# RWKV chunk inverse: four levels on the 32x32 diagonal squares, the last level as two products of the cross block

## What is computed

```python
def step(S, inp):
    r_t, w_t, k_t, v_t, kk_t, b_t = inp
    sa = jnp.einsum('bhij,bhj->bhi', S, -kk_t)
    S = (S * w_t[:, :, None, :] + sa[..., None] * b_t[:, :, None, :]
         + v_t[..., None] * k_t[:, :, None, :])
    return S, jnp.einsum('bhij,bhj->bhi', S, r_t)
...
y = (rwkv7_scan(r_h, heads(decay[:, :, 0]), k_h, v_h, kk, b_h, False)
     + rwkv7_scan(r_h, heads(decay[:, :, 1]), k_h, v_h, kk, b_h, True))
```

## Time and profile before

| | us |
|---|---|
| Median of 3 runs | 3145.51 (3141.09 to 3147.05) |
| The profiled execution | 3141.4 |
| Its span, from the first to the last instruction | 3139.6 |
| Stage `rwkv_mix` in it | about 568 to 987 |
| One turn of the stage in it | 23.4 and more |

### The profile page before, as it was taken

The page is one execution under the profiler, slowest core; times in us unless marked ns, Lnnn a source line. Parts: engine busy times, 40 slices in busy tenths (PEclk is TensorE's granted clock), DMA queues, the critical chain, the costliest instruction groups (busy, mean ns, idle before and its releaser), DMA issues.

```text
span 3139.6 us, 56591 instructions
## 1 busy us (share of the span) xinstructions
PE 2915.1 (93%) x25024; PEld 2375.0 (76%) x25024; DVE 1467.5 (47%) x2046; ACT 1153.1 (37%) x1897; POOL 280.8 (9%) x318
## 2 busy tenths in 40 slices
PE   6986899688888799999999999999999999999997
PEld 5765666578785478888888887787887888888886
DVE  3668676245444454433343325666436533234323
ACT  5665665222223243322332225533234333243222
POOL 1000123444441100000000000000000000000000
PEclk8987899799998799999999999999999999999998
DMA  4320244311100222223222222222322223223222
GB/s 141 123 68 3 90 143 141 84 34 34 34 4 30 92 89 89 93 94 99 96 89 95 99 94 97 85 94 87 101 94 88 94 94 101 94 94 121 100 94 81
DMA packets 99541, 273.07 MB, mean 87 GB/s; under 512 B 8224, under 2 KB 35488, under 8 KB 99296
## 3 DMA queue, kind: packets, MB, share of 16 engines
q1 hardware_dynamic: 90512, 236.93, 22.9%
q0 software_dynamic: 8784, 32.51, 3.1%
HBM read 256.69 MB, written 12.58 MB: 86 GB/s over the span
## 4 chain that ended last, share of the span: by engine, by line
PE 62%; DVE 2%; ACT 1%; DMA 1%; issue 0%; DVEq 0%; ACTq 0%
PE be_ps L2921 45%; PE be_ps L2942 15%; DVE be_ring L2711 1%; PE be_ps L2955 1%; PE be_ps L2663 0%; PE be_ps L2657 0%; ACT be_whi L2988 0%; DMA be_raw<-in_w_out 0%; DVE be_raw_r L3094 0%; DMA be_raw<-in_ple_gate 0%; DVE be_total L2676 0%; DVE ext_r L2721 0%; ACT big L2994 0%; DVE big L2684 0%; DVE big L2693 0%
## 5 line engine op out<-in xcount | busy, mean ns | idle before, releaser
L3094 DVE TENSOR_TENSOR be_raw_r<-be_raw,be_whi 128x1024 fp32r<-128x1024 f32 x361 | 442.4, 1225 | 1002.9 <-ACT be_whi L2988 1002.6
L2921 PE MATMUL be_ps<-ext_r,be_whi 128*128 128x512 f32 x2304 | 714.1, 391 | 15.8 <-PEq L2331 8.6
L2988 ACT CAST be_whi<-be_raw 128x1024 fp32r<-128x1024 f32 x361 | 378.6, 1049 | 895.9 <-DMA be_raw<-in_ffn_down 317.1
L2921 PE MATMUL be_ps<-big_r,be_whi 128*128 128x512 f32 x2048 | 642.2, 394 | 2.4 <-DVE big_r L2719 2.4
L2921 PEld LDWEIGHTS be_ps<-ext_r,be_whi 128*128 128x128 f32 x2304 | 432.5, 188 | 109.0 <-issue 10.2
L2921 PEld LDWEIGHTS be_ps<-big_r,be_whi 128*128 128x128 f32 x2048 | 383.1, 188 | 96.7 <-DVE big_r L2719 3.1
L2921 PE MATMUL be_ps<-ext_r,be_raw_r 128*128 128x512 f32 x1152 | 449.3, 390 | 0.0
L2921 PE MATMUL be_ps<-big_r,be_raw_r 128*128 128x512 f32 x1024 | 407.5, 398 | 0.0
L2942 PE MATMUL be_ps<-ext_r,be_whi 128*128 128x512 f32 x1152 | 354.6, 389 | 0.0
L2921 PEld LDWEIGHTS be_ps<-ext_r,be_raw_r 128*128 128x128 f32 x1152 | 217.0, 188 | 45.3
L2942 PEld LDWEIGHTS be_ps<-ext_r,be_whi 128*128 128x128 f32 x1152 | 216.3, 188 | 45.0
(11 more groups left out here) (328 smaller groups left out, 3886.8 us busy)
## 6 DMA issues: line engine op xcount, KB each, us to landing
be_raw<-in_ffn_gate SPq DMA_DIRECT2D x88, 512.0 KB, 3.5
be_raw<-in_ffn_up SPq DMA_DIRECT2D x88, 512.0 KB, 3.5
be_raw<-in_ffn_down SPq DMA_DIRECT2D x88, 512.0 KB, 3.5
be_raw<-in_conv_in SPq DMA_DIRECT2D x48, 512.0 KB, 3.5
gp_ada<-in_ada POOLq DMA_DIRECT2D x24, 512.0 KB, 3.8
rp_ada<-in_ada POOLq DMA_DIRECT2D x24, 512.0 KB, 3.8
rwkv_prepared<-big SPq DMA_DIRECT2D x16, 512.0 KB, 3.1
be_raw<-in_w_out SPq DMA_DIRECT2D x16, 512.0 KB, 3.6
```

What stands on the lines that cost most here:

```text
L2921: mm = pe.matmul(ps[:, bank], part[:, k * P:(k + 1) * P], xs(k), start=(k == 0 and i == 0), stop=(k == KD - 1 and i == 2))
L2988: act.copy(w.hi[:, n % 3], w.raw[:, n % 3]).then_inc(w.hi_ready, 1)
L3094: dve.tensor_tensor(w.lo(n), w.raw[:, n % 3], w.hi[:, n % 3].bitcast(F32), ALU.subtract).then_inc(w.lo_ready, 1)
```

## The change

Levels 1 to 4 work within the 32x32 squares on the diagonal alone, since all blocks up to 32 rows lie there. `x`, `xt0`, `mx` and the new `xt_sq` hold only these squares (32 columns for each tile in place of 64). Each product of these levels becomes 8 tiles x 4 squares = 32 matmuls, with a stationary operand of 32x32 and 16 moving columns. The fifth level becomes two products of the cross block: the first square's `x` against 32 rows and all 64 columns of `mp` (`cross`), a DVE copy, then the result against the second square's `xt_sq` (`crossed`), and a DVE copy into `xt`. One more DVE operation (`own`) puts the diagonal squares into `xt`. Both products have 16 matmuls, with a stationary operand of 32x64 and 32 moving columns. On POOL `xt0` is made of two halves and their sum. The masks of the levels are half as wide, and only one tile (`cross`, before five of `mx`) is filled with the unit matrix at the stage's start.

```diff
@@ masks @@
-        for n, s in enumerate(LEVELS[1:6]):
-            col = np.arange(CH).reshape(CH // (2 * s), 2, s)[:, d].reshape(1, -1)
-            off = (row // (2 * s) == col // (2 * s)) & (row // s != col // s)
-            out[:, CONST["level_m"] + 2 * n + d] = np.tile(off | (row == col), 4)
+        out[:, CONST["first_rows"], d:d + 1] = p // SQ % 2 == d
+        for n, s in enumerate(LEVELS[1:5]):
+            col = np.arange(SQ).reshape(SQ // (2 * s), 2, s)[:, d].reshape(1, -1)
+            off = (p % SQ // (2 * s) == col // (2 * s)) & (p % SQ // s != col // s)
+            out[:, CONST["level_m"] + n, d * CH:(d + 1) * CH] = np.tile(off | (p % SQ == col), 4)
@@ rwkv_mix, helpers @@
-    levels = range(1, 6)
+    levels = range(1, 5)
+        def cross_one(c, first, d, h, q):
+            at = first + (h * 2 + q) * SQ
+            return ps[chunks[c], LX + d, at:at + SQ]
+        def crosses(first):
+            return ps[:, LX:LX + 2, first:first + 4 * SQ].rearrange("p d (k s) -> p d k s", s=SQ)
+        def square(e):
+            return slice(SQ * e, SQ * e + SQ), slice(SQ * (e % 2), SQ * (e % 2) + SQ)
@@ POOL, first_inverse @@
-                pool.tensor_tensor(xt0[:, :].rearrange("p d h q t -> p d (h q) t"),
-                                   mp[:, par].rearrange("p d h q t -> p d (h q) t"),
-                                   pairs_t.rearrange("p d (a t) -> p d a t", a=1).to_broadcast([P, 2, 4, CH]), ALU.mult
-                                   ).then_inc(*pool_front("xt0"))
+                for name, dst, cols in (("xt0_first", xt0, slice(0, SQ)), ("xt0_more", xt0_more, slice(SQ, CH))):
+                    pool.tensor_tensor(dst[:, :].rearrange("p d h q t -> p d (h q) t"),
+                                       mp[:, par, :, :, :, cols].rearrange("p d h q t -> p d (h q) t"),
+                                       pairs_t[:, :, cols].rearrange("p d (a t) -> p d a t", a=1).to_broadcast([P, 2, 4, SQ]),
+                                       ALU.mult).then_inc(*pool_front(name))
+                pool.wait_ge(*pool_front.by("xt0_more", t))
+                pool.tensor_tensor(flat(xt0), flat(xt0), flat(xt0_more), ALU.add).then_inc(*pool_front("xt0"))
@@ PE, turn @@
-                    for d in two:
-                        for h in heads:
-                            for q in two:
-                                for c, at in enumerate(chunks):
-                                    ins = mm(compact_one(LX, at, 0, n, d, h, q), mp[at, par, d, h, q],
-                                             joined_one(x[at, d, h, q], n, d))
+                    for d, h, q in tiles:
+                        for e in range(4):
+                            rows, cols = square(e)
+                            ins = mm(compact_one(rows, 0, n, d, h, q), mp[rows, par, d, h, q, cols],
+                                     joined_one(x[rows, d, h, q], n, d))
                     ins.then_inc(*pe_made(f"mx{n}"))
...
+                pe.wait_ge(*act_made.by("x4", t))
+                for d, h, q in tiles:
+                    for c in two:
+                        first, _ = square(2 * c + d)
+                        ins = mm(cross_one(c, 0, d, h, q), mp[first, par, d, h, q], x[first, d, h, q])
+                ins.then_inc(*pe_made("cross"))
+                if ahead:
+                    front_v(*divmod(t + 1, n_turns), t + 1)
+                pe.wait_ge(*dve_made.by("cross", t))
+                for d, h, q in tiles:
+                    for c in two:
+                        second, _ = square(2 * c + 1 - d)
+                        ins = mm(cross_one(c, 4 * SQ, d, h, q), cross[second, d, h, q], xt_sq[second, d, h, q])
+                ins.then_inc(*pe_made("crossed"))
+                pe.wait_ge(*pe_made.by("ya0", t))
+                to_output(par, 0, qk)
@@ DVE, turn, behind level 4 @@
+                dve.wait_ge(*pe_made.by("cross", t))
+                dve.tensor_copy(joined(cross[:], 5), crosses(0)).then_inc(*dve_made("cross"))
+                dve.wait_ge(*dve_made.by("xt4", t))
+                dve.tensor_tensor(joined(xt[:], 5), xt_sq[:, :].rearrange("p d h q t -> p d (h q) t"), spread_rows(first_rows),
+                                  ALU.mult).then_inc(*dve_made("own"))
+                if ahead:
+                    front_x(t + 1)
+                if j >= n_turns // 2:
+                    bonus(g, j, t)
+                dve.wait_ge(*pe_made.by("crossed", t))
+                dve.tensor_copy(joined(xt[:], 5, True), crosses(4 * SQ)).then_inc(*dve_made("xt"))
```

More of the change, by code:

```diff
@@ L1699, in rwkv_mix @@
         ak, qk = by_kappa[:, :, :, :, :, 0], by_kappa[:, :, :, :, :, 1]
-        xt0 = sb("xt0", [P, 2, 2, 2, CH])
-        x = sb("x", [P, 2, 2, 2, CH])
+        xt0, xt0_more, x, xt_sq = (sb(f"{n}", [P, 2, 2, 2, SQ]) for n in ("xt0", "xt0_more", "x", "xt_sq"))
+        mx = sb("mx", [P, 4, 2, 2, 2, SQ])
+        cross = sb("cross", [P, 2, 2, 2, CH])
         xt = sb("xt", [P, 2, 2, 2, CH])
-        mx = sb("mx", [P, 5, 2, 2, 2, CH])
         nv = sb("nv", [P, 2, 2, 2, CH])
@@ L1791, in rwkv_mix @@
         pe_made = Marks(core.sem("rw_pe"), ["mx1", "rhs0", "xx1", "ya0"] +
-                        [f"{s}{n}" for n in levels[1:] for s in ("mx", "xx")] +
+                        [f"{s}{n}" for n in levels[1:] for s in ("mx", "xx")] + ["cross", "crossed"] +
                         ["u0", "end0", "y0", "rhs1", "ya1", "u1", "end1", "y1"])
@@ L1795, in rwkv_mix @@
         dve_made = Marks(core.sem("rw_dve"), ["mx1", "rhs0", "xt1"] + [f"{s}{n}" for n in levels[1:] for s in ("mx", "xt")] +
-                         ["u0", "state0", "rhs1", "u1", "state1"])
+                         ["cross", "own", "xt", "u0", "state0", "rhs1", "u1", "state1"])
         pool_made = Marks(core.sem("rw_pool"), ["kept0", "kept1"])
@@ L1893, in turn @@
             def turn(g, j, t, par, ahead):
-                for n in levels[:4]:
+                for n in levels:
                     act.wait_ge(*pe_made.by(f"xx{n}", t))
-                    act.copy(joined(x[:], n), compact(LX, 4 * CH, n)).then_inc(*act_made(f"x{n}"))
+                    act.copy(joined(x[:], n), compact(4 * SQ, n)).then_inc(*act_made(f"x{n}"))
                     if n == 3 and ahead == 2:
@@ L2143, in turn @@
             def turn(g, j, t, par, ahead):
+                tiles = [(d, h, q) for d in two for h in heads for q in two]
                 for n in levels:
@@ L2165, in turn @@
                         front_beta_tok(t + 1)
-                    elif ahead and n == 5:
-                        front_v(*divmod(t + 1, n_turns), t + 1)
                     pe.wait_ge(*dve_made.by(f"mx{n}", t))
-                    for d in two:
-                        for h in heads:
-                            for q in two:
-                                for c, at in enumerate(chunks):
-                                    old = (xt0 if n == 1 else xt)[at, d, h, q]
-                                    if n < 5:
-                                        ins = mm(compact_one(LX, at, 4 * CH, n, d, h, q), old,
-                                                 joined_one(mx[at, n - 1, d, h, q], n, d))
-                                    else:
-                                        ins = mm(compact_one(LT, at, 0, n, d, h, q), mx[at, n - 1, d, h, q],
-                                                 joined_one(old, n, 1 - d))
+                    for d, h, q in tiles:
+                        for e in range(4):
+                            rows, _ = square(e)
+                            ins = mm(compact_one(rows, 4 * SQ, n, d, h, q), (xt0 if n == 1 else xt_sq)[rows, d, h, q],
+                                     joined_one(mx[rows, n - 1, d, h, q], n, d))
                     ins.then_inc(*pe_made(f"xx{n}"))
@@ L2228, in _ @@
             eyes = eye.rearrange("p (a t) -> p a t", a=1)
-            for n in range(5):
-                ins = dve.tensor_copy(mx[:, n].rearrange("p d h q t -> p (d h q) t"), eyes.to_broadcast([P, 8, CH]))
-            ins.then_inc(eyes_ready, 1)
+            dve.tensor_copy(cross[:, :].rearrange("p d h q t -> p (d h q) t"), eyes.to_broadcast([P, 8, CH])).then_inc(eyes_ready, 1)
             def front_out(t, par, name):
```

51 lines of the change are left out of this document (22 added, 29 removed).

## The result

The changed kernel takes 3278.22 us (median; 3276.87 to 3280.34), the kernel before in the same series 3146.1: a ratio of 1.0424, with an interval of 1.0406 to 1.0442. It is slower by 132 us where the forecast said 92.

A forecast was written before the change was run, and what follows sets the result against it. Instruction packets were to bound a `rwkv_mix` turn at 28.8 us, plus 1.7 for the clock, 30.5; over the stage, first and last turns included, 92 us more, so 3237 us (3190 to 3278).

The forecast's parts named there:

- 28.8 us: A turn of `rwkv_mix` at full clock: 7.75 instruction packets at 3.65 us, 28.3, plus 0.5 for dependent steps (27.6 to 30.0).
- the rival with packets that come early enough: In `rwkv_mix` the steps alone decide, 2.0 to 2.5 us saved a turn: 3113 us; faster by over 0.2%, chance 9%.
- Two signs: Foretold for `rwkv_mix`: one packet every 3.6 to 3.9 us, and PE idle for "issue" 80 us and more.
- 1.7 us a turn (0 to 3): Clock term: half clock lengthens 6 us of PE work, fifth level and steps behind it, by 0.7 for two fifths of the time.
- the last turn: Last turn of `rwkv_mix`, 28 us: 6.25 packets make 23, plus 2 for the clock, so 3 us less.
- The step that failed: Clock of `rwkv_mix` inferred from PE's busy share falling from 87% to about 61%, by two stretches with clocks 0.71 and 0.63.
- Where PE waits for packets this hides: Claim that half clock's longer products in a turn cost nothing beside packet waits, only in the fifth level and steps behind.
- PE stays at half clock: Rival: most of `rwkv_mix` at 0.5 clock, a turn of 33 us or more: 3278 us and up, chance 8%.
- The steps' own gains: Shorter products, mask and copy in levels 1 to 4, less shape changes and `bonus`: 2.0 to 2.5 us a turn.
- A change of shape: PE switching between matmul shapes: 0.13 us seen, 20 changes a turn, half meeting a wait, 1.0 us a turn back.
- turn of 21.2: Length of a `rwkv_mix` turn in us that the steps alone would want, without packets as a bound.
- The cross products: Fifth level: two products of 1.1 us kept, a copy of 0.42 in place of a mask of 0.42: no change.

The follow-up runs named there:

- wide64: The changed kernel with the products of levels 1 to 4 moving 64 columns instead of 16, still 496 matmuls a turn: 3253.42 us, ratio 1.0353.
- half_columns: The kernel before, with its products of levels 1 to 4 moving only the first 16 of their 32 columns: 3181.46 us, ratio 1.0119.
- more16: The kernel before plus 16 matmuls of 4 columns ahead of each product of levels 1 to 4, 496 a turn: 3452.43 us, ratio 1.0972.
- twice: The kernel before with each product of levels 1 to 4 issued twice at the full 32 columns, 496 matmuls a turn: 3289.02 us, ratio 1.0476.
- half_wide64: The changed kernel with products of levels 1 to 4 for every other tile only, moving 64 columns, 368 matmuls a turn: 3145.89 us, ratio 1.0008.
- last_alone: The kernel before with only the fifth level as in the changed kernel, levels 1 to 4 untouched: 3145.25 us, ratio 1.0003.
- half_tiles: The changed kernel with products of levels 1 to 4 for every other tile only, from the second turn, 368 matmuls a turn: 3185.65 us, ratio 1.0124.

## Why the forecast was right or wrong

**Direction right, and the packets are a bound where the clock is full.** "Each packet takes at least 3.5 to 3.8 us, I take 3.65 [...] 28.8 us" is what the four turns of `wide64` at full clock show, 28.8 in the mean, though with longer products than the forecast had. 7.76 packets a turn and long stops inside the products, each ended by a packet, are as foretold, and the rival with packets that come early enough is out. The closest two packets in 620:960 are 3.32 us apart, a little under the 3.5 that I called the least. Two signs did not come: a packet every 3.6 to 3.9 us (it is 4.26 in the mean), and 80 us and more of stops: 48.9 by PE's records and 74.2 by PEld's in 460 us. Both say that in the changed kernel itself the packets are not the only bound.

**The size: wrong, in one term, the clock.** I put 1.7 us a turn (0 to 3) on the 28.8; measured are 33.05, so **4.2**, some 2.5 more. Over fourteen turns that is some 36 of the 40 us that are missing; some 3 more are the last turn, which was to get 3 us shorter and took 27.7 us (last copies at 1086.76 and 1114.51) for 27.4 before (951.47 and 978.90). The step that failed reads "its busy share falls from 87% to about (20.5 - 2.8) / 28.8 = 61%. Two stretches show what comes then". It took the clock for a function of the busy share, and read "two fifths of the time" at half clock from two stretches with 65% and 79% busy. It also let the half clock lengthen only the 6 us of PE work behind the inverse. In the trace after, the busy share is 85% and the clock is at half for four fifths of the time. `half_columns` at 90% and `more16` at 96% busy have 0.85 and 0.60. What these kernels differ in from before is how many columns a matmul moves, not how long PE is busy; `wide64` and `twice` show it from the other side. Here a rule of the Trainium skill misleads too, or at least isn't enough: TensorE: Matmul & The Clock Gate ("Why this matters for your kernels") asks that TensorE be kept busy, without long idle gaps, for the full clock. The traces of `more16` and `half_columns` have no stop over 0.7 us in the 340 us and lose the clock all the same; the measurement decides.

The second half of that step, "Where PE waits for packets this hides", was only partly true. At half clock, PE's own work of a turn is about as long as its 7.75 packets, so one does not hide the other. A turn of the changed kernel adds up so: 390.14 / 13.9 = 28.1 us busy, 3.5 for packets, and 19.1 / 13.9 = 1.4 for ACT and DVE, 33.0 in all. So without any stop it would be some 29.5 us at its clock, and at full clock 28.8 by its packets (both estimates): each of the two alone would have cost some 5 of the 9 us, and taking one away would have left the other. As I read the stops, PE has about one packet in hand after a stretch in which it is the slower one, and in the 7 us at full clock it runs that down and stops, for 1.6 us at 734.75 and 3.6 at 769.91. 3.5 us of stops a turn are left in the changed kernel, for 4.8 (51.4 / 10.7) in `wide64`.

I had this outcome as a rival, "PE stays at half clock", with 33 us and "3278 and up", at 8%. Both the turn and the time came out as that rival gave them, the cause (half clock for most of the stage) too; that its sum, 28.8 and 6 us of PE work at 1.7 times, hits 33.0 is in part luck, since the trace adds up otherwise. The chance was too small because I judged it by the busy share.

**The steps' own gains: right, and worth little.** Foretold 0.75 for a product at full clock, measured 0.73; mask 0.29 and 0.29; ACT's copy 0.27 and 0.27; transpose 0.43 and 0.45. By the floor for start-to-start in the Trainium skill (TensorE: Matmul & The Clock Gate, "Wait — 56ns, not 53.3ns?") the forecast's estimate was 1.6 us; the trace has 0.73. A change of shape costs 0.11 to 0.15 us at full clock where neither side waits (the last record of one form to the first of the next, in most cases), near the 0.13 of the forecast. The "turn of 21.2" without packets and at full clock has no kernel of its own. The nearest is the shortest turn of `half_wide64`, 21.4, whose products take 0.65 instead of 0.73, which makes 22.0 (an estimate): the steps gave at least 0.8 us a turn less than I had summed, and where these went was not followed up. The cross products cost nothing, as said (`last_alone`).

**What stays open.** How the clock depends on the work was not settled beyond the rows above. In the changed kernel the clock falls just where PE has small products and stops at once, and none of the runs has stops without small operands; that the fall comes without stops is shown, that stops add nothing to it is not. Nor does the forecast's reading, that the next packet is asked for when PE enters the one that has landed, explain why the packets ahead of the longest stops start so late: the one in 767.3:767.5 came 7.7 us behind the one before, when PE had already stood since 766.3. `wide64` (32x32 weights, 51.4 us of stops) has 0.87 and `twice` (64x64 weights, 3.6 us) 0.92, and which of the two differences makes this one was not separated. Nor was it tried to give the changed kernel full clock without touching its products.

## What to carry to other kernels

Count instructions and not only work: where PE is faster than its packets, smaller tiles in twice the number of matmuls pay for each with its share of an instruction packet, here some 3.65 us for 64 matmuls in fp32. And don't look for the clock in the busy share: with small moving operands PE was busy for more than nine tenths of the time and at 1.2 GHz for most of it (`more16`: 96%, 0.60), and then everything on it, the untouched steps too, takes up to 1.7 times as long. When two bounds lie close together, as the packets and the half clock here, expect little from lifting one of them. Before shrinking an operand, look whether its columns cost anything (here 16 and 32 columns took the same time, and 4 nearly); if they don't, the smaller one buys nothing and may cost the clock.

## What was not expected of the hardware

- Adding columns that nobody reads made the changed kernel 25 us faster (64 for 16 columns), and `half_tiles` 40 us faster (3185.65 to 3145.89). Taking half of them away in the products of levels 1 to 4 made the kernel before 39 us slower.
- The duration of a matmul group of 64x64 weights did not depend on 16 or 32 columns: 1.11 and 1.12 us for 32 records at full clock. With 32x32 weights on four places, 16 columns take 0.73 for 64 records and 64 columns 1.11.
- 64 records of 32x32 weights last 0.73 us at full clock, so they start at most 12 ns apart in the mean, closer than the 25 ns of the same section of the Trainium skill (TensorE: Matmul & The Clock Gate, "Wait — 56ns, not 53.3ns?") that the forecast weighed.
